# Sparing a small-matmul stretch its modulation products, and fusing two of its products, in a hybrid recurrent trunk on one Trainium2 core

## The chip, the cores and the metric

The kernel runs on one core of one Trainium2 chip. The time is device time in microseconds (us) from start to end of one execution; before and after are compared by the medians of several runs. The engines are named as in the profile: PE (TensorE matmuls), PEld (its weight loads), DVE (VectorE), ACT (ScalarE), POOL (GpSimd), SP (SyncE, here the queue that issues nearly all DMAs).

## The reference: what is computed

Two layers over 320 tokens: one prompt of 256 and 8 sample sequences of 8. All is float32, D_MODEL is 1024. Cut to what matters:

```
mods = (silu(c) @ ada_w + ada_b)                       # per layer 9 x 1024 columns, for 3 sub-layers
x = residual(x, 0, swiglu(modulate(x, 0), ...), 0.5)    # first feed-forward, FF = 2752
proj = modulate(x, 1) @ w_in
o_rw  = RWKV-7 over 6 heads of 64    # chunks of 64 tokens, states S (64x64) per head and sequence
o_gla = gated linear attention, 4 heads, 48 x 96
o_ml  = mLSTM, 4 heads of 64         # numerator and denominator from s @ v and C, n
mix = concat(o_rw, o_gla, o_ml) @ w_out
x = residual(x, 1, mix, 1.0)
x = residual(x, 2, swiglu(modulate(x, 2), ...), 0.5)    # second feed-forward
```

`modulate` needs the shift and scale columns of `mods`, `residual` its gate columns and a layer norm. For the sample sequences the RWKV part starts from a given state Z0 and needs, for each head and sequence, Z0 times R (the output's part that comes from the state) and Z0 times W (which goes into U, the solved inner values).

## The kernel before, in words

Tokens lie in the free dimension (320 columns), features on the 128 partitions. Every large product is done in three passes over split operands (`whi`, `wlo` are the two parts of a weight chunk, made by ACT and DVE from `raw`). Weights come as chunks of 512 KB through a ring `raw` of four buffers (RAW = 4), in the order `LOADS`, all issued by SP. A buffer is loaded again once its chunk is used: SP waits on `lo_done` for a dense chunk, on `ada_used` for a modulation chunk. In the gap of a product (the layer norm behind it) up to six modulation chunks (AHEAD = 6) come through a ring of their own, `raw_own`, which lies over memory of the mixers and so waits for their stores.

The order of work is a list, `PLAN`, that PE, ACT and DVE all walk through in the same order, each doing its own part of a step. `layer_plan` writes it: first feed-forward, `down`, `norm`, the 31 projection tiles, the nine RWKV steps that prepare its inputs, then the mixers, `out`, `norm`, second feed-forward. The steps of RWKV, GLA, mLSTM and of the sample states' update are called `rw`, `gl`, `ml`, `su`.

The modulation, 72 chunks in each layer, is filler: a step `ada` is one chunk (four matmuls with 256 columns each in `ada`, L1881); four chunks are a group, summed in one PSUM bank. When the fourth is done ACT copies the bank to `MR` (L2088), and a step `fold` (L1891, two matmuls of 18 columns, then `unfold` on DVE, L2161) puts the group's columns into `MODS`. While a layer's RWKV steps go on, all groups use one bank, psC, since psY is RWKV's; the first chunk of a group waits until ACT has copied the group before it.

The mixers have two parts. The **first** has 19 `rw` steps, from the transposes (L680) and scores (L690) over the doubling steps of the triangular inverse (`six`, L701, in which PE's products and DVE's masked adds take turns) to W, RB (L730, L740) and U (L748), with seven `ml` and `gl` steps between. The **second** has 12 `rw` steps for the chunks of the prompt's recurrence (L765 to L787, outputs L821 and L823) and the samples (L797, L802, L810), with the rest of `gl`, `ml` and `su`. It ends with the head norms and `mix`. Behind it stand three `rw` steps and `out`.

In the plan before, the modulation steps `ada` and `fold` are spread evenly over both parts. Layer 0 has 8 groups there (32 chunks), layer 1 has 6 (24 chunks). The lines of the samples and of mLSTM that the change touches are L797, L802 (96 separate matmuls of 8 columns) with the copy `GT` on ACT (L906), and L1472 (mLSTM's products of scores and values, in four turns of ten matmuls; after the first five and after the last five of a turn PE waits for its own last matmul, `rt.after`), L1478 and L1483.

The printed functions below are those the change touches, with the lines of the profile.

## Time and profile before

| | |
|---|---|
| median of 3 runs | 1860.99 us (1849.41, 1860.99, 1867.94) |
| profiled execution | 1865.12 us, span of its instructions 1863.3 us |
| PE busy | 1722.8 us (92%) |
| DVE, ACT, POOL busy | 975.1, 674.8, 170.4 us |
| mean granted TensorE clock | 0.906 of full speed |
| DMA | 270.24 MB, mean 145 GB/s |

The span is what the profile's times count from. Times of steps below are read in that one execution; the two layers run the same steps, some 900 us apart, so that each stretch can be read twice. A granted clock of 1.00 is 2.4 GHz, of 0.50 is 1.2 GHz. In a group's tile, as 64\*64, stand the rows and columns of the array that it takes. A float32 matmul shows as two records.

### The profile page before, as it was taken

What the parts mean: (1) busy time and instruction counts of PE and PEld (TensorE: products, weight loads), DVE (VectorE), ACT (ScalarE), POOL (GpSimd) and SP (SyncE); (2) the same over time, 40 slices, a digit from 0 to 9 for tenths busy, and PEclk for the clock granted to TensorE, in tenths of its full rate; (3) what the DMA queues carried; (4) which work ended last, traced back from release to release, by engine and by line L of the source; (5) the groups of instructions that cost most, each with busy time, mean ns of one, the idle gap of its engine ahead of it and who ended that gap; (6) DMA issues with size and microseconds to landing.
All of it is one profiled execution on the core that took longest, in us unless ns stands there. A gap on an engine that the chain in (4) does not pass through costs nothing.

```text
span 1863.3 us, 33349 instructions
## 1 busy us (share of the span) xinstructions
PE 1722.8 (92%) x14324; PEld 1553.6 (83%) x14324; DVE 975.1 (52%) x1627; ACT 674.8 (36%) x945; POOL 170.4 (9%) x217
## 2 busy tenths in 40 slices
PE   5999999989899789999999999999879986899997
PEld 2899998987778568999989999988867764799997
DVE  2444446585633467555464445458564346655544
ACT  2223335463211435433353333355432123533333
POOL 1000012002001022000120000110020011300011
PEclk9999999999855589999999999999998557999999
DMA  8555664433232135444635555643323212344442
GB/s 329 174 202 211 195 215 138 153 102 114 93 121 68 48 120 214 148 148 153 220 120 203 186 189 172 214 144 113 113 70 122 68 49 80 110 158 153 151 147 74
DMA packets 92370, 270.24 MB, mean 145 GB/s; under 512 B 27168, under 2 KB 29504, under 8 KB 91968
## 3 DMA queue, kind: packets, MB, share of 16 engines
q1 hardware_dynamic: 87808, 265.50, 41.9%
q10 hardware_dynamic: 4416, 2.62, 0.5%
q8 instruction: 113, 1.85, 0.4%
q14 instruction: 33, 0.27, 0.0%
HBM read 261.83 MB, written 6.26 MB: 144 GB/s over the span
## 4 chain that ended last, share of the span: by engine, by line
PE 79%; DVE 13%; ACT 4%; DMA 2%; issue 2%; POOL 0%; SPq 0%; DVEq 0%; ACTq 0%; POOLq 0%
PE psV L1866 11%; PE psV L1868 11%; PE psV L1867 11%; PE psA L1866 9%; PE psA L1868 8%; PE psA L1867 8%; PE psC L1881 2%; PE psV L701 2%; DVE wlo L2151 2%; DMA raw<-weights_dram 2%; ACT whi L2027 1%; DVE PJ L1387 1%; PE psV L1891 1%; PE psY L1881 1%; PE psV L1472 1%
## 5 line engine op out<-in xcount | busy, mean ns | idle before, releaser
L2151 DVE TENSOR_TENSOR wlo<-raw,whi 128x1024 fp32r<-128x1024 f32 x340 | 420.0, 1239 | 441.4 <-ACT whi L2027 438.8
L2027 ACT ACTIVATE whi<-raw 128x1024 fp32r<-128x1024 f32 x340 | 358.0, 1055 | 332.9 <-PE psV L1868 324.5
L1866 PE MATMUL psA<-XH,whi 128*128 128x320 f32 x1200 | 383.2, 319 | 34.3 <-DVE XL L2203 23.6
L1867 PE MATMUL psA<-XL,whi 128*128 128x320 f32 x1200 | 374.9, 312 | 0.0
L1868 PE MATMUL psA<-XH,wlo 128*128 128x320 f32 x1200 | 374.5, 312 | 0.0
L1866 PEld LDWEIGHTS psA<-XH,whi 128*128 128x128 f32 x1200 | 229.1, 191 | 55.2 <-issue 34.4
L1866 PE MATMUL psV<-XH,whi 128*128 128x320 f32 x816 | 259.9, 319 | 14.7 <-DVE wlo L2151 7.2
L1867 PE MATMUL psV<-XL,whi 128*128 128x320 f32 x816 | 256.6, 314 | 0.0
L1868 PE MATMUL psV<-XH,wlo 128*128 128x320 f32 x816 | 256.3, 314 | 0.0
L1867 PEld LDWEIGHTS psA<-XL,whi 128*128 128x128 f32 x1200 | 229.5, 191 | 0.3
L1868 PEld LDWEIGHTS psA<-XH,wlo 128*128 128x128 f32 x1200 | 229.1, 191 | 0.0
L1866 PE MATMUL psV<-HH,whi 128*128 128x320 f32 x704 | 217.4, 309 | 0.0
L1868 PE MATMUL psV<-HH,wlo 128*128 128x320 f32 x704 | 217.3, 309 | 0.0
L1867 PE MATMUL psV<-HL,whi 128*128 128x320 f32 x704 | 217.3, 309 | 0.0
L1866 PEld LDWEIGHTS psV<-XH,whi 128*128 128x128 f32 x816 | 157.4, 193 | 28.9 <-issue 24.1
L1867 PEld LDWEIGHTS psV<-XL,whi 128*128 128x128 f32 x816 | 157.7, 193 | 0.0
L1868 PEld LDWEIGHTS psV<-XH,wlo 128*128 128x128 f32 x816 | 157.3, 193 | 0.0
L1867 PEld LDWEIGHTS psV<-HL,whi 128*128 128x128 f32 x704 | 132.0, 188 | 0.0
L1866 PEld LDWEIGHTS psV<-HH,whi 128*128 128x128 f32 x704 | 132.0, 188 | 0.0
L1868 PEld LDWEIGHTS psV<-HH,wlo 128*128 128x128 f32 x704 | 132.0, 188 | 0.0
L2112 ACT ACTIVATE SG<-psA 128x320 f32<-128x320 f32 x84 | 36.7, 437 | 220.5 <-PE psA L1868 220.5
L2274 DVE TENSOR_TENSOR HF<-SG,psV 128x320 f32<-128x320 f32 x84 | 41.0, 488 | 85.1 <-PE psV L1868 85.1
(378 smaller groups left out, 1947.5 us busy)
## 6 DMA issues: line engine op xcount, KB each, us to landing
raw<-weights_dram SPq DMA_DIRECT2D x456, 512.0 KB, 3.3
raw_own<-weights_dram SPq DMA_DIRECT2D x24, 512.0 KB, 5.5
raw<-weights_dram SPq DMA_DIRECT2D x8, 256.0 KB, 3.7
ZS<-st_rw_dram SPq DMA_DIRECT2D x2, 768.0 KB, 4.4
S<-st_gla_dram ACTq DMA_DIRECT2D x2, 768.0 KB, 5.4
o_glas_dram<-S SPq DMA_DIRECT2D x2, 768.0 KB
o_rws_dram<-ZS SPq DMA_DIRECT2D x2, 768.0 KB
CON<-consts_dram SPq DMA_DIRECT2D x1, 1288.5 KB, 10.6
```

The source lines that it names most:

```text
L701: ins = mm(bank[c, h * CH:(h + 1) * CH], lhs, rhs, start=True, stop=True)
L1387: V.do(stt(out, x(tap), pcol("conv_w", 4 * tap + i), out, ALU.mult, ALU.add))
L1472: ins = mm(bank[p, tc:tc + CH], VM[c, tau, h, part], ST[c, tau, h], start=(tau == 0 and half == 0), stop=False, skip_group_check=True)
L1866: mm(out, whi[:, n % SPL, k], hi[:, kt], start=first, stop=False)
L1867: mm(out, whi[:, n % SPL, k], lo[:, kt], start=False, stop=False)
L1868: return mm(out, wlo[:, n % SPL, k], hi[:, kt], start=False, stop=last)
L1881: ins = mm(psM[BANK[group]][o:o + 32, 0:256], CT[:, 2 * q + k], w[:, k, half], start=(q == 0), stop=(q == 3))
L1891: ins = mm(bank[:, 18 * j:18 * j + 18], MR[:, n % 2, j * P:(j + 1) * P], FOLD[:], start=True, stop=True)
L2027: activation(whi[:, n % SPL], buffer(DENSE[n]), ACT.Copy).then_inc(hi_done, 1)
L2112: A.do(activation(SG[:, u % 2], bank[:, 0:TOK], ACT.Silu), sem("gate_done"))
L2151: tt(wlo[:, n % SPL], buffer(DENSE[n]), whi[:, n % SPL].bitcast(F32), ALU.subtract).then_inc(lo_done, 1)
L2274: V.do(tt(HF[:, u % 2], SG[:, u % 2], bank[:, 0:TOK], ALU.mult), sem("hidden_done"))
```

## The change

Four edits. (1) All `ada` and `fold` steps of the mixers stand in their first part, none in the second. (2) In layer 1, two of the six groups (8 chunks) leave the mixers altogether and go into the gap of the second `out`, the layer norm, where layer 0 already has two groups; their folds follow in the feed-forward behind it. (3) For the sample states, R and W are laid side by side in WT[2], so that one matmul of 16 columns gives both products; the W half is read by ACT out of psY, behind the whole product and not behind the W products alone. ACT copies R into WT[2] in the first part. (4) mLSTM's L1472 opens both banks of a head pair at once and lets the two heads of the pair, on opposite halves of the array's rows, alternate; it waits for its own last matmul twice for each pair of heads and no longer four times.

```
-    together += spread([(rw[0], 1)] * (RW_CHUNKS + RW_SAMPLES - 1), other)
-    out += spread([(step, 1) for step in together], ada_groups(in_tail) if in_tail else [])
+    out += spread([(step, 1) for step in together], ada_groups(in_tail))
+    out += spread([(rw[0], 1)] * (RW_CHUNKS + RW_SAMPLES - 1), other)
...
-    steps, left = layer_plan(1, groups(1, 1, 0, 1, 2, 3), (groups(1, 1, 4, 5), [], []), groups(1, 2, 0, 1, 2, 3, 4, 5), left)
+    steps, left = layer_plan(1, groups(1, 1, 0, 1, 2, 3), (groups(1, 1, 4, 5), groups(1, 2, 4, 5), []), groups(1, 2, 0, 1, 2, 3), left)
...
                         pe.wait_ge(*at("rw_state", 16))
-                        bank = bA.open()
+                        pe.wait_ge(*at("rw_wr", 2))
                         for h, s in PAIRED[:RW_H * DB]:
                             j, p = hp(h)
-                            ins = mm(bank[p, j * NS + 8 * s:j * NS + 8 * s + 8], ZS[p, j, s],
-                                     WT[tau][p, j, 8 * s:8 * s + 8], start=True, stop=True)
-                        f = bA.close(ins)
-                        for h, s in PAIRED[:RW_H * DB]:
-                            j, p = hp(h)
-                            ins = mm(psY[p, j * P + 8 * s:j * P + 8 * s + 8], ZS[p, j, s],
-                                     AR[p, 1, j, t0 + 8 * s:t0 + 8 * s + 8],
+                            ins = mm(two(psY[:, 0:RW_W], p, j, s), ZS[p, j, s], two(whole(WT[tau]), p, j, s),
                                      start=(s == 0 and j == 0), stop=False, skip_group_check=True)
-                        rt.after(ins)
+                        ins.then_inc(sem("rw_g_full"), 1)
                         yield
-                        pe.wait_ge(*f)
+                        pe.wait_ge(*at("rw_gt", 1))
...
+            def two(t, p, j, s):
+
+                return t[p, j * P:(j + 1) * P].rearrange("p (x t) -> p x t", x=2)[:, :, DS * s:DS * (s + 1)]
...
-                    A.do(activation(WT[tau][:, :, 0:w], bank[:, 0:RW_W].rearrange("p (j t) -> p j t", t=P)[:, :, 0:w], ACT.Copy),
+
+                    o = P - w
+                    A.do(activation(WT[tau][:, :, o:P], bank[:, 0:RW_W].rearrange("p (j t) -> p j t", t=P)[:, :, 0:w], ACT.Copy),
                          sem("bankA_free"))
+                A.do(activation(WT[2][:, :, 0:NS], AR[:, 1, :, SEQ:TOK], ACT.Copy), sem("rw_wr"))
+                A.mark(sem("rw_wr"))
...
-                        bank = fA.take()
-                        A.do(activation(GT[:], bank[:, 0:RP * NS].rearrange("p (j t) -> p j t", t=NS), ACT.Copy), sem("bankA_free"))
+                        act.wait_ge(*at("rw_g_full", 1))
+                        A.do(activation(GT[:], psY[:, 0:RW_W].rearrange("p (j t) -> p j t", t=P)[:, :, NS:P], ACT.Copy), sem("rw_gt"))
...
-                    for part in (slice(64, 128), slice(0, 64)):
-                        bank = bV.open()
-                        for half in range(2):
-                            if half:
-                                rt.after(ins)
-                            for h in (2 * j, 2 * j + 1):
-                                _, p = hp(h)
-                                for tau in range(3 - half):
-                                    c, tc = PARTS[tau][half]
-                                    ins = mm(bank[p, tc:tc + CH], VM[c, tau, h, part], ST[c, tau, h],
-                                             start=(tau == 0 and half == 0), stop=False, skip_group_check=True)
+
+                    parts, banks = (slice(64, 128), slice(0, 64)), []
+                    for _ in parts:
+                        banks.append(bV.open())
+                        bV.close()
+                    for turn in range(2):
+                        for tau in range(3):
+                            for bank, part in zip(banks, parts):
+                                for i, h in enumerate((2 * j, 2 * j + 1)):
+                                    half = (turn + i) % 2
+                                    if half == 0 or tau < 2:
+                                        _, p = hp(h)
+                                        c, tc = PARTS[tau][half]
+                                        ins = mm(bank[p, tc:tc + CH], VM[c, tau, h, part], ST[c, tau, h],
+                                                 start=(tau == 0 and turn == 0), stop=False, skip_group_check=True)
                         rt.after(ins)
+                    for bank, part in zip(banks, parts):
...
-                        bV.close(ins)
+                        ins.then_inc(sem("bankV_full"), 1)
```

Within the first part the 32 chunks of layer 0 now stand partly in pairs; between the last chunk of a group and the first of the next there is no other step at three of its seven boundaries; eight chunks stand directly behind another one. Layer 1 has 16 chunks there, none directly behind another. The order of the DMAs is the same in layer 0.

## Rows read from the trace of the kernel before

**Rows 1.** The page: the granted clock in 40 slices of 46.6 us; the ending chain by engine

```profile
PEclk9999999999855589999999999999998557999999
...
PE 79%; DVE 13%; ACT 4%; DMA 2%; issue 2%; POOL 0%; SPq 0%; DVEq 0%; ACTq 0%; POOLq 0%
```

**Rows 2.** Windows: layer 0's first part, second until its head norms, and its end; layer 1

```profile
438.00:519.80 81.80, 70.11 (x1280) 57.39 (x1279) 45.99 (x86) 24.75 (x46) 13.58 (x9) 0.83 0.30 98
519.80:612.10 92.30, 90.68 (x1068) 69.75 (x1067) 32.94 (x77) 9.19 (x20) 7.63 (x5) 0.52 0.28 90
612.10:651.70 39.60, 29.06 (x292) 17.94 (x291) 16.63 (x27) 19.74 (x21) 4.53 (x4) 0.54 0.19 57
1349.00:1422.70 73.70, 59.95 (x1244) 49.25 (x1242) 46.41 (x85) 24.49 (x45) 13.57 (x9) 0.95 0.24 79
1422.70:1511.00 88.30, 86.69 (x1044) 67.49 (x1042) 31.51 (x75) 8.93 (x19) 7.63 (x5) 0.53 0.27 84
```

The columns are the stretch, its length, busy us (with the count) of PE, PEld, DVE, ACT, POOL, then granted clock, DMA share and GB/s.

**Rows 3.** Windows of the same stretches, line 1881 (modulation chunks, eight records each) alone

```profile
438.00:519.80 81.80, 10.03 (x120) 2.40 (x120) 0.83 0.30 98
519.80:612.10 92.30, 13.62 (x108) 2.58 (x108) 0.52 0.28 90
...
1349.00:1422.70 73.70, 7.03 (x88) 1.73 (x88) 0.95 0.24 79
1422.70:1511.00 88.30, 11.00 (x88) 2.11 (x88) 0.53 0.27 84
```

**Rows 4.** Windows, line 1891 (folds, four records each) alone

```profile
519.80:612.10 92.30, 2.79 (x12) 2.87 (x12) 0.52 0.28 90
1349.00:1422.70 73.70, 1.24 (x8) 1.04 (x8) 0.95 0.24 79
```

**Rows 5.** Timeline, ACT and PE: a group's copy; a chunk at half clock, its follower

```profile
521.77 0.38 ACT L2088 ACTIVATE MR<-psC 128x256 f32<-128x256 f32 x1 [1.26 <-PE psC L1881]
...
523.22 1.08 PE L1881 MATMUL psC<-raw,CT 128*32 128x256 f32 x8
524.23 0.69 PE L1156 MATMUL psA<-CON,PJ 128*128 128x128 f32 x2
```

**Rows 6.** Waits of PE in layer 1's first part: who for whom, us, times, longest

```profile
PE psV L701 <- DVE Yb L1051: 4.5, 2, 3.4
```

**Rows 7.** Timeline, PE: the same 30 matmuls of 64 columns in layer 0 and layer 1

```profile
515.91 4.08 PE L748 MATMUL psA<-RB,Tt 64*64 64x64 f32 x60
...
1420.32 2.47 PE L748 MATMUL psA<-RB,Tt 64*64 64x64 f32 x60
```

**Rows 8.** Timeline, PE: ten matmuls of GLA and ten of mLSTM, at half clock

```profile
563.22 2.50 PE L1197 MATMUL psA<-ATG,VG 64*96 64x64 f32 x20
...
571.89 1.93 PE L1472 MATMUL psV<-ST,VM 64*64 64x64 f32 x20
```

**Rows 9.** Timeline, PE, ACT and DVE: sample products, the norm's root, and its user

```profile
621.83 3.14 PE L797 MATMUL psA<-WT,ZS 64*64 64x8 f32 x96
624.83 4.59 PE L802 MATMUL psY<-AR,ZS 64*64 64x8 f32 x96
...
629.25 1.27 ACT L614 ACTIVATE PJ<-PJ 96x1280 f32<-96x1280 f32 x1
...
630.69 1.48 DVE L1318 TENSOR_TENSOR PJ<-PJ 96x1280 f32<-96x1280 f32 x1
```

**Rows 10.** Timeline, PE: the gap behind `out`, layer 0 with chunks, layer 1 without

```profile
709.93 1.93 PE L1881 MATMUL psC<-raw_own,CT 128*32 128x256 f32 x32
...
715.95 0.39 PE L1866 MATMUL psA<-XH,whi 128*128 128x320 f32 x1 [1.96 <-DVE XL L2203]
...
1607.40 0.70 PE L1964 MATMUL psV<-SQ,CON 128*128 128x320 f32 x2
...
1614.15 0.61 PE L1866 MATMUL psA<-XH,whi 128*128 128x320 f32 x1 [6.05 <-DVE XL L2203]
```

**Rows 11.** Window with eight modulation loads in flight; columns as in the windows above

```profile
696.00:706.00 10.00, 10.00 (x70) 10.00 (x69) 4.56 (x10) 3.99 (x6) 4.42 (x6) 1.00 1.01 407
```

More of the change, by code:

```diff
@@ L281 @@
     rw_spread_u=3, rw_spread_v=3, rw_gsq=1, rw_xs=NRW, rw_kk0=1, rw_n2=1, rw_root=1, rw_b=2, rw_exp=4, rw_be=1, rw_yc=1, rw_gvar=1,
-    rw_gsd=1, rw_m=1, rw_mh=1, rw_su=3, rw_inverse=1, rw_shift=16, rw_shift_kept=2, rw_am=3, rw_u8=1, rw_zs=3, mixed=MIXT,
+    rw_gsd=1, rw_m=1, rw_mh=1, rw_su=3, rw_inverse=1, rw_shift=16, rw_shift_kept=2, rw_am=3, rw_u8=1, rw_zs=3,
+    rw_wr=2, rw_g_full=1, rw_gt=1, mixed=MIXT,
     gl_start=1, gl_hats=1, gl_state=NCH + 1, gl_state0=16, gl_kx=1, gl_sq=1, gl_abs=1, gl_log=1, gl_b=2, gl_exp=3, gl_ot=1, gl_out=1,
```

## Prediction

> **What bounds the kernel now.** I read the page first. PE carries 79% of the chain that ended last, and its granted clock is full nearly everywhere but in two places, the slices at 5 and 7, which are the mixers of the two layers [rows 1]. The change touches only these (and one gap behind them), so the windows came next, cut at steps that both layers have: the first part (L680 to U, L748), the second part until the prompt's last output (L823), and the end with the head norms up to the first product behind `mix` [rows 2]. The reader is to see three kinds of work. In the first part of layer 0 PE works 70.1 of 81.8 us; the rest are waits for DVE, which takes turns with it in the inverse. In the second part PE works 90.7 of 92.3 us at a granted clock of 0.52: it is bound by PE, and each instruction there costs about double. At the end PE works 29.1 of 39.6 us and neither DVE nor ACT is full: a chain that crosses the engines. The modulation's filler stands in all three [rows 3]. So the question is not how much work is taken away (nearly none is) but where it costs least.
>
> Whole run: span 1863.3 us in a profiled execution of 1865.1 us, 1.8 us outside; that execution lies 4.1 us above the median of 1861.0. The sum is made against 1865.1 and carried over to the median in proportion.
>
> **Prices of the filler.** At half clock a chunk's record is 1.08 us, and the next matmul starts 1.01 us after it [rows 5]; so its tail overlaps by 0.07 us and it costs 1.01 us. In layer 1's first part 11 chunks take 7.03 us, 0.64 each; less the tail, 0.57 us at full clock [rows 3]. A fold costs 2.79/3 = 0.93, less the tail 0.86 us at half clock, and 1.24/2 = 0.62, less the tail 0.55 us at full [rows 4]. Four chunks in a row take 1.93 us [rows 10], 0.47 each and not 0.57: a chunk directly behind another saves 0.1 us. The Trainium skill (TensorEngine Tiling (Array Packing), Key Properties) says that a change of the tiling mode drains TensorE; a chunk takes 128\*32 tiles and its neighbours 64\*64, so it would be this switch that a second chunk spares, and the trace agrees in sign, with 0.1 us. The sum takes the rows' number.
>
> **Second part, edits 1 and 2: gain.** Layer 0 has 13 chunks between 519.8 us and L823's end (the 14th, in the window by half, stands behind it). One of them is in the few us at full clock: 12 × 1.01 + 0.57 = 12.7, and 3 folds 2.6: 15.3 us. Layer 1 has 11 (11.00 us of records is nine at 1.08 and two at 0.64): 9 × 1.01 + 2 × 0.57 = 10.2, and 2 folds 1.8 us: 12.0 us. All of it lies on PE's path, since PE is 98% busy there and the list of its waits in these two stretches is empty. What it covered may come out as waits: DVE works 32.9 of 92.3 us there and ACT 9.2 [rows 2], and mostly one or two steps of another mixer, 2 to 5 us long, stand between a product and the step that needs its result. I take 1 us of new waits for each layer; the ends are 0 and 3 us.
>
> **End: nearly nothing.** Layer 0 has 4 chunks there, layer 1 two. The chain goes from L1216 over L1490, L797, ACT's copy GT and root (L614, to 630.52) to DVE (L1318, from 630.69) [rows 9], and on through DVE's state updates. Only what stands before L797 and behind L1216 is on it: one chunk in layer 0 (1.0 us), one fold at full clock in layer 1 (0.5 us). The rest is beside DVE; that PE is idle for 10.5 of 39.6 us says so too [rows 2].
>
> **First part: the cost.** Layer 0's is 81.8 us long with 15 chunks and 3 folds, layer 1's 73.7 with 11 and 2. Four chunks and a fold are 2.8 us of the 8.1 between them; the other 5.3 us are the clock, 0.83 against 0.95 [rows 2]: L748's 30 matmuls take 4.08 us in layer 0 and 2.47 in layer 1 [rows 7]. I take layer 1's as the base, since more filler means fewer stretches in which PE stands, and let layer 0's clock be a bound. Layer 0 then has 32 chunks and 8 folds: 73.7 + 21 × 0.57 + 6 × 0.55 = 89.0. Eight chunks behind another save 0.8. At three group boundaries with nothing between, PE waits for ACT's copy of psC: some 0.1 to ACT, 0.38 the copy [rows 5], and some 0.2 back (ACT to DVE took 0.17 [rows 9]), 0.6 us, 1.8 in all. Behind the waiting first chunk queue all of PE's following steps, so DVE's next masks wait too. Against that stand PE's waits in layer 1's first part, 73.70 − 59.95 = 13.75 us. The filler can use a wait only where it stands just before it: one chunk more before the first level (0.6), two chunks and a boundary for a fold before the second level's second half, where PE waits 3.4 us for DVE [rows 6] (1.2), about 1.1 before the third level's second half, 0.6 behind the last level, about 1 among the scores: 4.5 us. So 89.0 − 0.8 + 1.8 − 4.5 = 85.5, +3.7 us. Ends: all 13.75 used, 76.3 (−5.5); no wait used and layer 0's old clock, 81.8 + 17 × 0.57 + 5 × 0.55 + 1.8 − 0.8 = 95.2 (+13.4). Layer 1 goes to 16 chunks and 4 folds: 5 × 0.57 + 2 × 0.55 = 3.9, less 1.1 for waits used: +2.8; ends −2 and +5.
>
> **The loads.** SP issues the same loads in the same order, now wanted faster: 28 chunks (four lie ready) in some 85 us, 3.0 us each or 173 GB/s. The window with eight such loads in flight moved 407 GB/s [rows 11], 1.3 us each. I cost them at nothing. When they are used up SP goes on to the dense chunks of `out` and stands at the store of GLA's state, with nothing behind it that is wanted before `mix`.
>
> **Edit 2 in the gap.** Layer 0 shows it: its eight chunks lie inside the norm. From the first of them at 709.93 to the first matmul of the feed-forward are 6.0 us, and layer 1, without chunks, waits 6.05 us for DVE there [rows 10]. The chunks are free; the first matmul behind the gap is a record of 0.39 us in layer 0 and of 0.61 in layer 1 [rows 10], the clock having fallen, and some six groups of three matmuls at such a price are about 1 us that layer 1 should get back. Its two folds cost 2 × 0.55 = 1.1 us where PE is the bound. Sum 0. The loads now make SP wait for the mixers' stores in layer 1, and the weights of the feed-forward queue behind it; in layer 0 the same wait costs nothing that I can see. Ends −1 and +3 us.
>
> The Trainium skill (TensorE: Matmul & The Clock Gate, HAM oscillation) speaks against edit 1: it ties TensorE's clock to its being kept busy, so taking filler out of a stretch should cost clock. The trace bears it out in the gap. In the second part it does not: 98% busy, and half clock.
>
> **Edit 3.** On PE it takes 48 matmuls out of each layer. L797 started 3.0 us before L802, 0.0625 us for each of 48 at the clock granted there; L802's 4.59 us are 0.09 each [rows 9]. With 16 columns in place of 8 I expect no more, the weight load being the same. But the chain of the end passes L797 and not L802, which ended 1.3 us before DVE's L1318 could begin: what is saved is beside ACT. And ACT's copy now waits for all 48 products of psY: 3.0 us as before if the clock is as before, 4.5 at L802's pace, which is +1.5. I take +0.3 for each layer; ends 0 and 1.5. ACT's new copy of R and its mark stand where ACT has nothing to do until L748's products are there.
>
> **Edit 4.** A turn of ten matmuls takes 1.93 us [rows 8]. L748's, which alternate like the new ones, take 4.0/30 = 0.13 us each at half clock [rows 7], so the turn is 1.3 for ten and 0.3 for each of its two waits. New: 20 × 0.13 + 2 × 0.3 = 3.2 us for a pair of heads and not 3.86; two pairs, −1.3 us for each layer, on PE's path. Ends: −2.5 with the waits at nothing; +2.3 if ten take 2.50 as GLA's do [rows 8], which have the new order but 96 columns of weights. I take L748, whose tiles are the same. DVE's first bank is full later, its last one no later.
>
> **Sum.** Layer 0: +3.7 − 15.3 + 1.0 − 1.0 + 0.3 − 1.3 = −12.6. Layer 1: +2.8 − 12.0 + 1.0 − 0.5 + 0.3 − 1.3 + 0 = −9.7. Together −22.3 us, 1842.8 in the profiled execution; in proportion (1.2%) 1838.7 against the median, rounded to 1838.5. With the ends of the large terms it goes from 1824 to 1850.
>
> **Rivals.** (a) The gain is given back in the first part: every added chunk also delays DVE's next turn, so no wait is used, and layer 0 keeps its clock of 0.83. That is +13.4 and +5, and with 3 us of new waits in each second part −22.3 + 9.7 + 2.2 + 4 = −6: 1855. For it: the two engines do take turns, and filler between r and r+1 delays both. Against: layer 0 already has four chunks more than layer 1 and pays little else than the clock. (b) By the skill's rule above: with the filler gone the second parts lose the few us at full clock at their start (layer 1's average is 0.53, not 0.50), and the samples' product runs at L802's pace. 0.06 of 88 us is some 5 us at full clock that become 8, in each layer 3, and 1.2 each from edit 3: +8, 1847. (c) The other way: a denser first part hands over the full clock, and it lasts 20 us longer in each second part. L748 shows 2.47 for 4.08, 39% less: −7.8 each, 1823. Against: PE stands full in both second parts, and the clock is 0.52 and 0.53. (d) Slower: the loads of layer 0. If the ring of four could bring only what the first part shows now, 98 GB/s [rows 2], a chunk is 5.35 us, 28 are 150 us, and its first part grows by 70 us: 1861 + 70 − 26 = 1905. It decides for slower than before from (81.8 + 26)/28 = 3.9 us a chunk, 136 GB/s. Against: that low rate is SP waiting for PE's use, and 407 GB/s is three times the need. (e) A part of the change does not do what it says: edit 3 is such a part in my sum already.
>
> **How the numbers follow.** A difference under about 1% (18.6 us) can't be told from none by a measurement of this kernel. Forecast 0.60 (four fifths of it below 1842.4, the line of 1%); (a) 0.20, within 1%; (b) 0.09, within 1%; (c) 0.06, faster; (d) 0.05, slower. Faster 0.48 + 0.06 = 0.54, same 0.12 + 0.20 + 0.09 = 0.41, slower 0.05. The range goes from 1818, below (c), to 1859, above (a), and leaves out (d).
>
> **What would show it.** In the profile after: no line 1881 between L748 and `mix`; the second parts at about 76 and 75 us with PE still over 95% busy at about 0.5; layer 0's first part at 85 us with a clock above 0.9 and PE over 90% busy; the ends within 1 us of before; L1472 near 3 us for a pair; the gap of layer 1 at 6.7 us still, with eight chunks in it. Wrong would make me: a second part that shrinks by much less than its filler, DVE named as PE's releaser there; a first part that grows by over 10 us; or DMA named as a releaser of L1881.

## The result and the profile after

The changed kernel takes 1838.08 us (median of 4 runs, 1834.91 to 1839.23); the kernel before took 1860.65 us beside it (4 runs, 1849.41 to 1867.94). The ratio is 0.987, 95% interval [0.983, 0.991]. The forecast was 1838.5 us. A second set of four runs of the changed kernel gave 1838.1 us, ratio 0.989 [0.982, 0.995].

The profiled execution has a span of 1837.4 us and a mean granted clock of 0.919. From its page, the granted clock in 40 slices (now of 45.9 us):

```profile
PEclk9999999999875599999999999999989557999999
```

The mixers are still the only two places without full clock [rows 1]. The windows of the same six stretches, in the columns of before (stretch, length, busy us of PE, PEld, DVE, ACT, POOL, granted clock, DMA share, GB/s): layer 0's first part, second part, end; then layer 1's.

```profile
439.90:525.60 85.70, 74.99 (x1428) 56.05 (x1428) 47.51 (x94) 26.43 (x51) 13.58 (x9) 0.94 0.53 180
525.60:604.60 79.00, 75.48 (x959) 64.13 (x958) 31.80 (x71) 8.16 (x17) 7.63 (x5) 0.52 0.13 40
604.60:641.20 36.60, 15.55 (x156) 9.54 (x155) 16.38 (x25) 19.36 (x20) 4.53 (x4) 0.59 0.00 1
1337.10:1414.90 77.80, 67.00 (x1289) 53.78 (x1287) 45.34 (x85) 25.41 (x48) 13.59 (x9) 0.89 0.26 90
1414.90:1486.40 71.50, 69.56 (x950) 59.70 (x950) 32.44 (x75) 7.78 (x16) 7.63 (x5) 0.55 0.15 44
1486.40:1524.10 37.70, 18.47 (x155) 10.52 (x156) 16.42 (x25) 19.36 (x20) 4.53 (x4) 0.59 0.00 0
```

Layer 1's end has no row among those of before; there it was

```profile
1511.10:1548.30 37.20, 23.59 (x276) 15.47 (x276) 16.92 (x28) 19.74 (x21) 4.52 (x4) 0.59 0.09 29
```

Against this and [rows 2], by lengths: layer 0 +3.9 −13.3 −3.0, layer 1 +4.1 −16.8 +0.5. That is −12.4 and −12.2 of the 25.9 us by which the span fell. The rest, −1.3 us, lies in the stretches around the mixers (+1.9 ahead of the first, −1.4 between them, −1.7 behind the second). What grew and what shrank is what the prediction said. PE's busy time in layer 0's second part fell from 90.7 to 75.5 us at a clock of 0.52 in both.

How far one profile can be trusted shows in the second one of the changed kernel (experiment 5). Its execution took as long (1838.9 us for 1839.2), but layer 0's first part is 88.2 us in it and not 85.7, and layer 1's second part 73.5 and not 71.5. A difference of some 2.5 us in one stretch, read from two single profiles, shows nothing by itself.

**The first part** holds the one surprise. The longest of PE's waits in it, layer 0 and then layer 1 (who waits for whom, us in all, times, longest):

```profile
PE psC L1889 <- ACT MR L2096: 4.7, 3, 3.6
...
PE psC L1889 <- ACT MR L2096: 4.7, 1, 4.7
```

L1889 is the modulation chunk (L1881 before), L2096 ACT's copy of the group's bank. The wait that the copy should cost is 0.6 us; in each layer one such wait is 3.6 or 4.7 us. The timeline shows it, layer 0's on PE, ACT and DVE (start, us, what, in brackets the idle time before it and who ended it), and layer 1's on PE last:

```profile
487.64 1.08 PE L1889 MATMUL psC<-raw,CT 128*32 128x256 f32 x8 [3.65 <-ACT MR L2096]
...
486.14 0.47 ACT L1521 ACTIVATE row<-row 4x320 f32<-4x320 f32 x1 [15.80 <-DVEq L326]
...
487.24 0.36 ACT L2096 ACTIVATE MR<-psC 128x256 f32<-128x256 f32 x1
...
480.84 0.47 DVE L1556 SCALAR_TENSOR_TENSOR LF<-row,row 4x320 f32<-4x320 f32 x1
...
485.84 0.20 DVE L1582 TENSOR_TENSOR row<-row,row 4x64 f32<-4x64 f32 x1
...
486.19 1.48 DVE L1054 TENSOR_TENSOR Yb<-psV,CON 128x384 f32<-128x384 f32 x3
...
1381.74 1.08 PE L1889 MATMUL psC<-raw,CT 128*32 128x256 f32 x8 [4.70 <-ACT MR L2096]
```

Read it from the middle. An mLSTM step of row operations, small ones in long order, occupies DVE from 480.84 to 486.04. ACT's part of that step (L1521) needs them, so ACT stands; its copy MR is the next thing in ACT's order behind that part (L1521 to L1523) and so stands behind a wait that has nothing to do with it. PE in turn can't open the next group in psC.

Before, PE waited at this place too, for DVE's Yb: 3.3 us in layer 0, 3.4 in layer 1 [rows 6]. Yb stands behind the same row operations (L1054, at 486.19 above), so the old wait and the new one have one cause. In layer 1 the open group had been copied well before. In layer 0 the copy was as late as it is now, but the next chunk to need it came only at 486.47. In the kernel before, layer 0:

```profile
481.71 0.36 ACT L2088 ACTIVATE MR<-psC 128x256 f32<-128x256 f32 x1
```

So most of the new wait stands where an old one stood. What comes on top is ACT's part with the copy, and the chunk (1.08 us), which now runs behind the wait and not inside it.

**The end** in layer 0, the merged product (L798) on PE, then ACT's copy GT and the root, then DVE's use of it:

```profile
611.72 2.98 PE L798 MATMUL psY<-WT,ZS 64*64 64x16 f32 x96
...
614.74 0.33 ACT L909 ACTIVATE GT<-psY 128x192 f32<-128x192 f32 x1 [1.60 <-PE psY L798]
615.09 1.28 ACT L613 ACT_TABLE_LOAD   x1
616.38 1.27 ACT L613 ACTIVATE PJ<-PJ 96x1280 f32<-96x1280 f32 x1
617.67 1.28 ACT L615 ACT_TABLE_LOAD   x1
618.97 1.27 ACT L615 ACTIVATE PJ<-PJ 96x1280 f32<-96x1280 f32 x1
...
620.27 1.49 DVE L1321 TENSOR_TENSOR PJ<-PJ 96x1280 f32<-96x1280 f32 x1 [7.95 <-ACT PJ L615]
```

48 matmuls of 16 columns take 2.98 us where 48 of 8 took 3.14 [rows 9]: the extra columns are free, and the second product's 4.59 us are gone. DVE starts 15.7 us into the end and not 18.6 (a chunk less and a higher clock ahead of L798 make most of that, see the account of the sum below). ACT waits 1.60 us for GT's input with the root still to do behind it: a chain that was not touched, and the next thing to try.

**The gap** of layer 1, on PE:

```profile
1582.87 0.70 PE L1972 MATMUL psV<-SQ,CON 128*128 128x320 f32 x2
1583.50 1.93 PE L1889 MATMUL psC<-raw_own,CT 128*32 128x256 f32 x32
1585.25 1.05 PE L1889 MATMUL psY<-raw_own,CT 128*32 128x256 f32 x16
1586.11 1.05 PE L1889 MATMUL psY<-raw,CT 128*32 128x256 f32 x16
1589.49 0.38 PE L1874 MATMUL psA<-XH,whi 128*128 128x320 f32 x1 [2.33 <-DVE XL L2211]
```

From the norm's last product to the feed-forward's first matmul are 6.62 us, with eight chunks in between; without them it was 6.75 [rows 10].

### The profile page after: what moved, and what is told of

Its sections match the earlier page's. It is cut to its first block, busy times and chain, and to the rows that moved or that the text cites. A ratio compares the mean times of both kernels' runs of the same rounds, so it can differ in the third digit from the quotient of the medians.

```text
span 1837.4 us, 32974 instructions
## 1 busy us (share of the span) xinstructions
PE 1685.9 (92%) x14132; PEld 1531.9 (83%) x14132; DVE 975.3 (53%) x1627; ACT 675.0 (37%) x947; POOL 170.5 (9%) x217
## 4 chain that ended last, share of the span: by engine, by line
PE 77%; DVE 14%; ACT 4%; DMA 3%; issue 2%; POOL 0%; ACTq 0%; SPq 0%; DVEq 0%; POOLq 0%
PE psV L1874 11%; PE psV L1876 11%; PE psV L1875 11%; PE psA L1874 9%; PE psA L1876 9%; PE psA L1875 9%; DVE wlo L2159 3%; DMA raw<-weights_dram 3%; PE psV L702 3%; PE psC L1889 2%; ACT whi L2035 1%; DVE PJ L1390 1%; PE psY L1889 1%; DVE ZT L2200 1%; PE psV L691 1%
```

## Experiments

"Changed kernel" is the kernel after; each ratio is to the kernel before, run on the same chip. Its times there had medians of 1863.4, 1863.0 and 1864.2 us.

**1. The edits one by one.** Three kernels: the plan alone (edits 1 and 2), the merged product alone (edit 3), mLSTM's pairs alone (edit 4), each the corresponding hunks of the diff above.

> The kernel before with edits 1 and 2 alone (all filler in the first part, eight chunks of layer 1 in the gap). My theory, that the gain is the filler's place: nearly all of the gain of the whole change, 20 to 23 us less than before (1838 to 1841), ends of the mixers as long as before, L1472 still 1.9 us a turn. Rival, that a good part comes from the two changed products (edits 3 and 4 took 48 matmuls and half of the waits out of each layer): only 12 to 16 us less.

> The kernel before with edit 3 alone (R and W of the samples in one product). My theory: the end chain passes only the part up to ACT's copy, so 0 to +2 us in all and within the noise; from the first record of the samples' product to the first product behind mix 29.5 to 31 us as before. Rival, that PE's work at the end counts: 3 to 4.5 us less for each layer there, 6 to 9 in all.

> The kernel before with edit 4 alone (mLSTM's heads alternate, half of the waits). My theory: twenty matmuls take 3.2 us and not 3.9 for a pair of heads, -0.7 for each of four pairs, -2.7 us in all, within the noise of a run; to be read from the records. Rival, GLA's pace: 5 us a pair, +4.6 us in all.

Measured, ten runs each: plan alone 1841.67 us, ratio 0.992 [0.989, 0.995]; merged product alone 1856.96, 0.997 [0.992, 1.002]; pairs alone 1851.07, 0.997 [0.993, 1.001]. So the plan carries most of the change (21.8 us below the kernel before on the same chip, where my theory had 20 to 23), and the two others by themselves can't be told from nothing by these medians.

The medians of the last two hide something, since their runs are as scattered as those of the kernel before. With edit 3 alone four runs took 1841.8 to 1842.7 us, one 1850.6 and five 1863.3 to 1868.7; with edit 4 alone three took 1837.9 to 1838.4, five 1850.5 to 1853.0, the others 1858.3 and 1863.1. The fastest of each lie 6 and 10 us below the fastest of the kernel before (1847.8). The profile of edit 3 is of one of its slowest executions, so what that edit is worth in a fast one is open. The plan alone shows no such scatter (1839.9 to 1846.3).

Windows of the plan alone, second parts:

```profile
525.70:606.40 80.70, 76.86 (x959) 64.78 (x958) 31.80 (x71) 8.16 (x17) 7.63 (x5) 0.52 0.13 39
...
1414.60:1490.20 75.60, 73.33 (x951) 62.67 (x950) 32.45 (x75) 7.77 (x16) 7.63 (x5) 0.53 0.14 41
```

Removing the filler takes 11.6 and 12.7 us of them; edit 4, which is the difference to the changed kernel, 1.7 and 4.1 us. Of that difference in layer 1 a part is the clock, 0.55 for 0.53: in the second profile of the changed kernel that stretch had 0.54 and 73.5 us, 2.1 less than here. Edit 4's own rows, a pair of heads at half clock, in the kernel before and in the changed kernel:

```profile
573.89 0.90 PE L1478 MATMUL psV<-QW,CP 64*64 64x64 f32 x12
...
576.26 1.90 PE L1472 MATMUL psV<-ST,VM 64*64 64x64 f32 x20
...
578.24 0.90 PE L1478 MATMUL psV<-QW,CP 64*64 64x64 f32 x12
```

```profile
571.65 0.36 PE L1479 MATMUL psV<-ST,VM 64*64 64x64 f32 x1
...
571.81 3.13 PE L1479 MATMUL psV<-ST,VM 64*64 64x64 f32 x39
575.00 0.90 PE L1486 MATMUL psV<-QW,CP 64*64 64x64 f32 x12
```

Before, a turn lasts 2.00 us from its first matmul (571.89 [rows 8]) to L1478 and the next one 1.98, 3.98 for the pair; after, 3.35. Twice per layer that is −1.3 us, the forecast's term.

The merged product alone looked costly in its profile. Layer 1's end grew to 41.3 us with the copy GT waiting 3.93 us, which seemed to be the price of waiting for all 48 products. A second profile of the kernel before (experiment 5) refutes it. First edit 3 alone, then the kernel before again, the product and GT:

```profile
1520.19 5.31 PE L798 MATMUL psY<-WT,ZS 64*64 64x16 f32 x96
...
1525.54 0.33 ACT L909 ACTIVATE GT<-psY 128x192 f32<-128x192 f32 x1 [3.93 <-PE psY L798]
```

```profile
1510.70:1552.10 41.40, 29.45 (x276) 20.55 (x276) 16.92 (x28) 19.74 (x21) 4.53 (x4) 0.50 0.09 26
...
1519.92 5.29 PE L797 MATMUL psA<-WT,ZS 64*64 64x8 f32 x96
...
1525.26 0.33 ACT L906 ACTIVATE GT<-psA 128x192 f32<-128x192 f32 x1 [3.92 <-PE psA L797]
```

At half clock the W products alone take as long (5.29 us) as the merged ones (5.31), GT waits as long, and the end is as long (41.4). The 4 us belong to the clock of that execution. In these two executions edit 3 adds nothing to the chain and takes nothing off it, which is against the rival of 3 to 4.5 us for each layer.

**2. Does the eight chunks' move pay?** The changed kernel with edit 2 undone: all six groups of layer 1 in the first part.

```
-... (groups(1, 1, 4, 5), groups(1, 2, 4, 5), []), groups(1, 2, 0, 1, 2, 3), left)
+... (groups(1, 1, 4, 5), [], []), groups(1, 2, 0, 1, 2, 3, 4, 5), left)
```

> The changed kernel with edit 2 undone: layer 1's six groups all in its first part, none in the gap. My theory: eight chunks and two folds more in layer 1's first part cost 8 x 0.57 + 2 x 0.55 = 5.7 us less what waits hide, 3.5 to 5 us; the gap behind out loses nothing in length, the two folds behind it (1.1) go and the first matmuls behind it are slow again (+1): 3 to 5 us more than the changed kernel in all. Rival, that the first part still has waits to give: 0 to 1 us more.

Measured: 1846.87 us (ten runs), ratio 0.992 [0.989, 0.996], 8.8 us more than the changed kernel, where I had expected 3 to 5. Layer 1's first part:

```profile
1332.90:1417.60 84.70, 70.88 (x1361) 54.55 (x1359) 45.52 (x91) 25.97 (x50) 13.58 (x9) 0.92 0.41 132
```

84.7 us against 77.8: eight chunks and two folds cost 6.9 us there, more than at full clock their own 8 × 0.57 + 2 × 0.55 = 5.7, and PE's idle time rose from 10.8 to 13.8 us. Its waits for MR grew from 4.7 to 5.8 us, and that for DVE ahead of W's first product (L731) from 0.7 to 3.5. So the added filler used no wait and made new ones, while in the gap the same chunks cost nothing. This profile is of an execution of 1841.7 us, the second fastest of the ten and only 2.5 us above the profiled one of the changed kernel: where the rest of the 8.8 us between the medians lies it does not show.

**3. Where should the filler stand, and what does it weigh?** Two kernels: in one all mixer filler stands in the second part, in the other it stands as in the changed kernel but its matmuls have 8 columns and not 256, so most of the modulation values of these groups are not computed.

```
-    out += spread([(step, 1) for step in together], ada_groups(in_tail))
-    out += spread([(rw[0], 1)] * (RW_CHUNKS + RW_SAMPLES - 1), other)
+    out += together
+    out += spread([(step, 1) for step in spread([(rw[0], 1)] * (...), other)], ada_groups(in_tail))
```

```
-    ins = mm(psM[BANK[group]][o:o + 32, 0:256], CT[:, 2 * q + k], w[:, k, half], ...)
+    ins = mm(psM[BANK[group]][o:o + 32, 0:n_cols], CT[:, 2 * q + k], w[:, k, half, 0:n_cols], ...)
```

> The changed kernel with all of that filler in the second part and none in the first. By my prices: layer 0's second part until the last prompt output grows by about 24 chunks x 1.01 + 6 folds x 0.86 = 29 us (the rest falls in the end), layer 1's by some 15, and the first parts shrink by 12 and 6 us to about 73 and 71: 22 to 28 us slower than the changed kernel, 1860 to 1866. Rival, that filler keeps the clock up (the chip's rule as the notes have it): the second part's clock rises above 0.6 with it and the loss is under 12 us.

> The changed kernel with the filler of the mixers' first parts cut to 8 of 256 columns: chunks are loaded, waited for and signalled as before, but the modulation values of those groups are not computed. Theory A, the filler costs PE's path its price less some 5 us of waits: layer 0's first part goes from 85.7 to about 74 to 77 us (a thin chunk still costs about 0.15), layer 1's from 77.8 to about 71. Theory B, the first part is set by the turns with DVE and the filler is hidden: layer 0's first part falls by under 4 us. Theory C, filler holds the clock: the granted clock of the first part falls below 0.85 and the stretch hardly shrinks.

Measured: all in the second part 1863.24 us (ten runs), ratio 1.002 [0.999, 1.005]; thin filler 1829.07 (2 runs), 0.983 [0.977, 0.989]. Windows of layer 0, first and second part, with the filler in the second; then the two first parts with thin filler:

```profile
437.30:510.60 73.30, 56.11 (x1150) 50.42 (x1149) 46.03 (x83) 24.20 (x44) 13.58 (x9) 0.87 0.01 2
510.60:612.70 102.10, 99.76 (x1171) 70.34 (x1173) 32.56 (x78) 9.98 (x23) 7.72 (x5) 0.55 0.44 142
```

```profile
437.50:518.90 81.40, 66.61 (x1429) 59.51 (x1428) 47.55 (x94) 26.41 (x51) 13.58 (x9) 0.85 0.56 189
...
1326.50:1400.70 74.20, 60.79 (x1290) 54.27 (x1288) 46.04 (x85) 25.20 (x48) 13.59 (x9) 0.86 0.28 94
```

The first kernel is the change turned round, and it costs 25 us against the changed one, within the 22 to 28 expected. Its two first parts, empty of filler, are 12.4 and 3.7 us shorter than the changed kernel's, its second parts 23.1 and 18.7 us longer: the same filler costs there over twice what it costs in the first part. By my prices the two second parts should have grown by 29 and 15 us; the sum holds (41.8) better than its two terms. The rival fell: the second parts' clock is 0.55 and 0.52, not above 0.6.

The second kernel says what the filler still weighs where it now stands: cutting 97% of its columns takes 4.3 and 3.6 us off the first parts, where theory A had 9 to 12 us in layer 0, B under 4 and C a clock below 0.85; B and C are near, and A fell. In layer 0 the chunks' own records fell by 12.5 us (19.7 to 7.2), PE's busy time by 8.4 (74.99 to 66.61), the stretch by 4.3. So about a third went to the rest of PE's work, which got slower with the clock (0.94 to 0.85), and a third became waits, those for MR among them (5.4 us, as the boundaries are still there). In layer 1 it is 7.0, 6.2 and 3.6 us, with the clock at 0.86 for 0.89.

That filler holds the clock up in a part where PE otherwise stands in waits is well borne out in layer 0: with the filler as the changed kernel has it seven profiles (two of the changed kernel, the plan alone, edit 2 undone, two banks, early root, and these two together) lie at 0.91 to 0.96, four with the 15 chunks of before at 0.83 to 0.91, that with none at 0.87. In layer 1 it is weaker: 0.89 to 0.93 with 16 chunks, 0.89 to 0.95 with the 11 of before, 0.82 with none. The Trainium skill (TensorE: Matmul & The Clock Gate, HAM oscillation) says that gaps in TensorE's work bring the clock down; the trace agrees here in the direction, with these numbers. In the second parts filler makes no such difference: layer 0's is at 0.55 with all of it (PE 98% busy) and at 0.52 without (96%), layer 1's at 0.52 with and 0.55 without. There the clock is low with hardly a gap in PE's work, which the page's rule doesn't give.

**4. What is left in the two places found.** Two kernels on top of the changed one. In the first, the groups of the first part's stretch take the banks psC and psY in turns (psY is wanted by RWKV only from the second part on), so that a new group need not wait for MR. In the second, ACT takes GLA's root directly behind the gate, and GT behind it.

```
-        _busy = any(("rw", L) in PLAN[:_n] and ("rw", L) in PLAN[_n:] for L in range(DEPTH))
+        _rw = [PLAN[:_n].count(("rw", L)) for L in range(DEPTH)]
+        _busy = any(len(RW_PRE) + RW_INVERSE <= _rw[L] < PLAN.count(("rw", L)) for L in range(DEPTH))
```

```
                 A.do(activation(... T_GR:T_GR + GH], ACT.Silu), sem("gl_gate"))
-                yield
                 act.wait_ge(*at("gl_var", 1))
                 rsqrt(A, GN[0:DV], sem("gl_sd"))
+                yield
                 yield
```

> The changed kernel, but the groups of the first part take psC and psY in turns (psY is RWKV's only in the second part). If PE's waits at group boundaries for ACT's copy (L1889 from MR, 4.7 us in layer 0's first part, up to 4.7 us at one place in layer 1's) cost the path: layer 0's first part 2 to 3 us shorter, layer 1's 1 to 2, 3 to 5 us in all. If they only stand in for waits for DVE that come anyway: under 1.5 us in all, and L702's waits for DVE return with 2 to 4 us.

> The changed kernel with one yield moved: ACT takes GLA's root (two table loads, Ln and Exp, 5.1 us) directly behind GLA's gate instead of behind mLSTM's square and the copy of the samples' W product. If the end is the chain ACT root, then DVE (L1321 on): DVE's L1321 starts some 3.5 us sooner, and each layer's end gets 3 to 4 us shorter, 6 to 8 us in all. If PE or the later state updates set the end: no change.

Measured, four runs each: two banks 1830.0 us, ratio 0.983 [0.979, 0.987]; early root 1823.64, 0.981 [0.976, 0.985]. Both beat the changed kernel's 1838.1, with little or nothing shared between the ranges; it ran on other chips, on which the kernel before took 1860.7 and 1864.2 us for 1863.0 on this one. Windows of the first parts with two banks, and the wait that has taken the place of MR's, in layer 1:

```profile
435.80:519.80 84.00, 74.72 (x1429) 57.11 (x1431) 47.49 (x94) 26.43 (x51) 13.59 (x9) 0.94 0.54 183
...
1327.40:1400.10 72.70, 64.43 (x1289) 51.36 (x1287) 44.18 (x85) 25.40 (x48) 13.58 (x9) 0.93 0.28 96
...
PE psV L703 <- DVE Yb L1055: 4.2, 2, 3.3
```

The waits for MR are gone from both lists. PE goes on to its next product a chunk earlier and stands there for DVE instead (3.3 us, as before the change). PE's idle time falls only from 10.7 to 9.3 us and from 10.8 to 8.3, for 4.7 us of waits for MR gone in each layer. Net −1.7 and −5.1 us; in layer 1 the clock is 0.93 for 0.89 as well. Layer 0's −1.7 is less than the changed kernel's own first part varies (85.7 and 88.2, and 84.3 in the early root's profile, the same up to there); layer 1's is more (77.8, 77.0 and 77.8). Each of the two cases that I had set out came true in part: the first parts got 6.8 us shorter in all, and the waits for DVE returned with 3.1 and 2.2 us.

Early root, the two ends, and layer 0's order on ACT and DVE:

```profile
598.60:630.40 31.80, 16.22 (x157) 9.80 (x156) 16.42 (x25) 19.13 (x20) 4.53 (x4) 0.61 0.00 1
...
1474.20:1506.00 31.80, 18.31 (x157) 10.74 (x156) 16.43 (x26) 19.13 (x20) 4.53 (x4) 0.55 0.00 1
...
608.13 1.27 ACT L615 ACTIVATE PJ<-PJ 96x1280 f32<-96x1280 f32 x1
...
609.93 0.31 ACT L909 ACTIVATE GT<-psY 128x192 f32<-128x192 f32 x1
...
609.43 1.49 DVE L1321 TENSOR_TENSOR PJ<-PJ 96x1280 f32<-96x1280 f32 x1 [2.79 <-ACT PJ L615]
```

Each end is 31.8 us long, −4.8 and −5.9, 10.7 in all where I had expected 6 to 8. The medians differ by 14.5 us and the two profiled spans by 18.1; 3.0 of these are layer 0's second part, at 0.55 and 76.0 us for 0.52 and 79.0, which no edit of this kernel touches, so what the edit itself brings is nearer the 10.7. DVE starts 10.8 us into the end and not 15.7. GT, which looked like the thing to hurry, leaves at 11.3 us where it left at 10.1, and nobody misses it. The clock in the ends stays at 0.55 to 0.61 and PE is idle half the time: it was a chain of ACT and DVE, as the prediction had it, but a chain that could be cut.

**5. Together, and the two kernels once more.** Two banks with early root; the same with no filler behind U (the last steps of the first part's spreading moved ahead of it), to spare PE the wait of 1.59 us for MR at the fold that stands ahead of the second part's first product; and the kernel before and the changed kernel unaltered.

```
-    out += spread([(step, 1) for step in together], ada_groups(in_tail))
+    out += spread([(step, int(n < len(together) - 1)) for n, step in enumerate(together)], ada_groups(in_tail))
```

> The changed kernel with two banks for the first part's groups and GLA's root early, together. If the two act in different stretches (first parts; ends), the gains add: root_early took about 14 us off the changed kernel and two_banks about 8, so 1814 to 1819. If a shorter first part only shifts the clock's fall into the second part: 1819 to 1825.

> As the one before, with no filler behind U (L749) either: the last chunk and fold stand before it. In the changed kernel PE waited 1.6 us for ACT's copy there in layer 0 and the granted clock was at half from the next matmul on; in layer 1 it stayed full for some 6 us. If that wait makes the clock fall: layer 0's second part 2 to 4 us shorter than in the one before. If the clock falls anyway in the second part's small matmuls: within 1 us of it.

> The changed kernel again. The runs of the kernel before lie in two groups, near 1849 (granted clock about 0.915) and near 1866 (about 0.902). If the change takes work out of a stretch whose clock is a matter of chance, its own runs lie in one group at 1835 to 1840. If it has both groups too, some runs lie near 1822 or near 1855.

> The kernel before, for a second profile. If the two groups of its times are the clock in layer 0's second part: a profile of the lower group shows that stretch at 73 to 80 us and a clock above 0.6, one of the upper group at 92 us and 0.52, with all other stretches alike within 2 us.

Measured: both 1823.87 us, ratio 0.982 [0.976, 0.989], no better than early root alone, so the gains did not add up to the 1814 to 1819 that I had expected, and the time lies in the range of the rival; without filler behind U 1829.05, 0.985 [0.977, 0.993]; changed kernel 1838.1; kernel before 1867.54 (8 runs), 1.002 [0.998, 1.006].

Without filler behind U layer 0's second part is 6.4 us shorter, but 2.9 of them are the chunk, the fold and the wait that stood at its start, and its first part is 8.1 us longer, PE waiting 4.2 us for DVE at W's first product. In layer 1 it is −2.5 and +10.0 us, with a wait of 6.6 us for DVE's Yb. Moving all of the first part's filler a little earlier costs more than the wait for MR did; whether that wait made the clock fall this kernel can't tell.

Layer 1's first and second part with both:

```profile
1325.60:1398.40 72.80, 64.53 (x1290) 51.46 (x1288) 44.14 (x85) 25.38 (x48) 13.57 (x9) 0.93 0.29 96
1398.40:1472.40 74.00, 72.06 (x950) 62.15 (x950) 32.44 (x75) 7.77 (x16) 7.63 (x5) 0.53 0.14 42
```

The first part keeps its gain of 5 us; the second, which has the same instructions, is 74.0 us at 0.53, for 71.5 at 0.55 in the changed kernel's first profile and 73.5 at 0.54 in its second. Against the early root alone the two first parts are 6.3 us shorter and the two second parts 3.9 us longer (77.4 for 76.0 in layer 0). Whether a shorter first part costs the second part some of its clock, or whether this is the scatter of single executions, these profiles don't decide.

**The times of the kernel before fall in two groups.** In the longest of those series, 31 runs, 13 took 1847.8 to 1854.1 us and 17 took 1863.1 to 1872.3; the mean clock is 0.912 to 0.918 in the first and 0.898 to 0.909 in the second. The changed kernel's eight runs lie between 1831.0 and 1839.2 and show no such split, nor do the plan's ten. So its gain is about 28 us against the upper group and about 11 against the lower; the medians compare it with the upper, which holds over half of the runs. Both profiles of the kernel before are of the upper one, and they agree within 0.2 us in layer 0's second part (92.3 and 92.2), as expected, but not within 2 us elsewhere: 2.3 in layer 1's first part, 4.2 in its end. Edit 4 alone, whose runs scatter in the same way (1838 to 1863), was profiled in an execution of 1838.4 us. Layer 0's second part there, and five us within it:

```profile
516.50:589.40 72.90, 71.37 (x1066) 56.82 (x1068) 32.75 (x77) 9.20 (x21) 7.63 (x5) 0.71 0.35 115
...
530.00:535.00 5.00, 4.88 (x104) 3.28 (x103) 1.62 (x4) 1.18 (x3) 0.00 (x0) 1.00 0.75 253
```

With all its filler it is 72.9 us long, 19 us shorter than in the profiles of the kernel before, since the clock stayed at 1.00 until 547 us. In the kernel before it falls at about 509, is at 0.83 in one window of five us and is at 0.50 from 525 on. That this also makes the lower group of the kernel before is argued from the size (some 0.014 of mean clock between the groups would be some 50 us at full and not at half clock) and not shown: no profile of it fell in that group. The mean clock is a rough measure here, too: 26 us near the start (20 to 46 us), in which PE works about 15 us either way, had 0.50 in the second profile of the changed kernel and 1.00 in its first, which is most of 0.912 for 0.919 at nearly the same time.

## Why the prediction was right

**The sum** said −22.3 us in the span; it is −25.9 between the two profiled executions, and the medians moved by 22.6. That the forecast of 1838.5 us was met within 0.5 us is luck: single stretches miss by up to 4.5 us, in both directions, and the median of the kernel before depends on how many of its runs fall in which of its two groups. By its terms, layer 0 and layer 1:

- *Second part*, filler −15.3 and −12.0, new waits +1.0 each, edit 4 −1.3 each: −15.6 and −12.3 in all. Measured −13.3 and −16.8, 30.1 for 27.9, and here a shortfall of 2.3 us and an excess of 4.5 cancel in part. In layer 0 PE's busy time fell by 13.8 us with the plan alone (90.7 to 76.9): the last chunk (0.64) and its fold still stand behind U, which I had counted as gone, so that my sign "no line 1881 between L748 and `mix`" failed in layer 0; in layer 1 a fold stands there. The waits are 1.6 us for MR at that fold and 0.6 for ACT, 2.2 and not 1.0. Edit 4 is −1.26 by its rows. Layer 1's excess is in part the clock, 0.55 for 0.53; the second profile of the changed kernel has 73.5 us there, −14.8.
- *First part*, +3.7 and +2.8. Measured +3.9 and +4.1, and between the second profiles of the two kernels +6.3 and +1.0, so that 0.2 us of error in layer 0 is luck again. PE's waits for MR are 4.7 us in each layer and not 1.8 and 0: I had priced the copy by its own length and asked whether PE had other work between, not what ACT's queue was standing behind. But they are not the boundaries' price, since they stand where PE waited for DVE before. Two banks took them away, and PE's idle time fell by 1.4 and 2.5 us. So a boundary's price was near the 1.8 in layer 0 and was missed in layer 1. With two banks layer 0 has 9.3 us of idle time, where layer 1 before had 13.75: 4.5 us of the old waits were used, as in the sum. The clock of layer 0 rose to 0.94, as taken. Layer 1's fell from 0.95 to 0.89, and PE's busy time there is 3.1 us above 59.95 + 3.9.
- *End*, −0.7 and −0.2. Measured −3.0 and +0.5. The chunk on the path was worth its 1.0 us; the rest in layer 0 is that L1498 ran at full clock (1.24 us for L1490's 2.50). Edit 3 costs 0 in the profiles, and with it 48 matmuls go that nobody waited for.
- *Gap* of layer 1, 0: 6.62 us for 6.75. That SP's loads wait for the mixers' stores shows nowhere.

**The rivals.** (a) fell: the second parts kept their gain and layer 0's first part did not keep its clock of 0.83. A part of it is true, though: experiment 2's eight further chunks used no wait. And layer 1's clock was 0.89 for 0.95, but one execution does not fix this: the kernel before taken again had 0.89 in layer 1's first part and 76.0 us, against which the changed kernel's cost there is 1.8 us. (b) fell, with 0.52 and 0.55 for 0.52 and 0.53. (c) did not come about in the changed kernel, but the objection to it, that PE stands full there and so the clock must be low, was no objection: with edit 4 alone the same stretch, as full, kept full clock for its first 30 us. Its chance of 0.06 rested on that objection. In the changed kernel layer 1's second part did start at full clock, and kept it for some 5 us only. (d) fell: 180 GB/s in layer 0's first part, above the 173 worked out as the need, and no DMA among the releasers of the chunks. (e) is true of edit 3, which brought nothing in the profiles, and in small of edit 1, with what it leaves behind U.

**What was right for a reason** is that the filler's price goes by its place: about 1 us a chunk in the second part (experiment 3: 41.8 us for some 37 chunks and 5 folds), less in the first and nothing in the gap. Experiments 2 and 3 moved the same filler, and the time followed: 1838 us as changed, 1847 with edit 2 undone, 1863 with all in the second part. "0.57 or less" in the first part holds only while there are waits to use: in experiment 2 eight chunks and two folds cost 6.9 us there for 5.7.

## What to carry to other kernels

Filler has a price for each place, and it is read from three rows: its record's length at the clock of that place, PE's idle time there, and who ends the waits. Before relying on a short copy to free a buffer, look at what its engine's queue stands behind at that moment, not at the copy's length, and at which older wait the new one replaces: 4.7 us of waits removed gave 1.4 to 2.5 us of idle time here. An earlier place in the order can be worth more than the work itself, as the early root was (11 us in the two ends, for one step moved). And where a kernel's times fall in groups, profile more than one execution before explaining a stretch, and compare groups and not only medians: two profiles of one kernel differed by 4 us in an end.

## What the runs showed of the hardware

- 48 float32 matmuls on 64\*64 tiles take as long with 16 columns as with 8: 2.98 for 3.14 us near full clock, 5.31 for 5.29 at half.
- The same 92 us of small matmuls with PE 98% busy ran at a clock of 0.52 in three profiles and at 0.71 in one. The edit of that kernel, mLSTM's products, does nothing before its first L1475 at 550.65 us, when the clock had already come down again.
- A root by two activations with a table load before each is 5.15 us on ACT (1.28 + 1.27 + 1.28 + 1.27, with 0.05 between). The Trainium skill (ScalarE: Activation LUTs, What ACT_TABLE_LOAD costs) gives about 1.28 us for the load and about 1.38 for a drain, 2.66 in all. The trace has the 1.28; the activation starts 0.01 us behind it, and no drain can be seen, neither ahead of the load nor behind it.
